# Feed-forward input loops: a gate block and its up block interleaved product by product

## The reference

```python
def swiglu_ffn(x, w_in, w_out):
    gate, up = jnp.split(x @ w_in, 2, axis=-1)
    return (jax.nn.silu(gate) * up) @ w_out

h = h + FFN_RES_WEIGHT * swiglu_ffn(rmsnorm(h, norm_ffn1[l]), ffn1_w_in[l], ffn1_w_out[l])
```

## Time and profile before

| | us |
|---|---|
| median of 3 runs | 2399.88 (2399.85 to 2400.62) |
| the profiled execution, whole time | 2398.54 |
| its span, first to last instruction | 2396.8 |
| its mean granted TensorE clock | 0.985 of full speed |

### The profile page before, as it was taken

The page is one execution under the profiler, slowest core; times in us unless marked ns, Lnnn a source line. Parts: engine busy times, 40 slices in busy tenths (PEclk is TensorE's granted clock), DMA queues, the critical chain, the costliest instruction groups (busy, mean ns, idle before and its releaser), DMA issues.

```text
span 2396.8 us, 27538 instructions
## 1 busy us (share of the span) xinstructions
PE 2303.6 (96%) x10522; PEld 1897.6 (79%) x10522; DVE 1075.4 (45%) x1093; ACT 736.1 (31%) x926; POOL 690.8 (29%) x485
## 2 busy tenths in 40 slices
PE   8999999999999999999999999997867899999997
PEld 7888888887777888888878888876767787888886
DVE  5444334534465454443454443356534435444333
ACT  4222222322323342222333222234321134322221
POOL 3444104501231034442124444011222212444300
PEclk9999999999999999999999999999989999999998
DMA  4333333333222333333333333331100012333332
GB/s 145 96 96 96 106 105 121 107 97 89 73 76 80 97 97 96 96 96 101 106 95 97 95 98 101 105 99 55 45 27 27 27 44 88 97 96 96 97 105 88
DMA packets 58817, 213.31 MB, mean 89 GB/s; under 512 B 6528, under 2 KB 6784, under 8 KB 58624
## 3 DMA queue, kind: packets, MB, share of 16 engines
q1 hardware_dynamic: 58464, 210.02, 28.3%
q0 software_dynamic: 288, 2.36, 0.3%
HBM read 210.26 MB, written 2.10 MB: 89 GB/s over the span
## 4 chain that ended last, share of the span: by engine, by line
PE 89%; DVE 4%; issue 3%; ACT 2%; POOL 2%; DMA 0%; POOLq 0%; DVEq 0%; SPq 0%
PE acc L465 27%; PE acc L466 27%; PE acc L467 27%; DVE c_acc L1636 1%; PE mixb L680 1%; PE mixb L698 1%; PE mixb L693 1%; PE mixb L860 1%; PE sums L495 1%; PE acc L804 1%; PE acc L803 1%; PE acc L802 1%; ACT w_hi L929 0%; POOL r_raw L1771 0%; PE mixb L840 0%
## 5 line engine op out<-in xcount | busy, mean ns | idle before, releaser
L465 PE MATMUL acc<-x_hi,w_hi 128*128 128x512 f32 x2016 | 803.2, 398 | 10.0 <-DVE x_lo L1262 9.0
L467 PE MATMUL acc<-x_hi,w_lo 128*128 128x512 f32 x2016 | 788.4, 391 | 0.0
L466 PE MATMUL acc<-x_lo,w_hi 128*128 128x512 f32 x2016 | 788.2, 391 | 0.0
L465 PEld LDWEIGHTS acc<-x_hi,w_hi 128*128 128x128 f32 x2016 | 381.6, 189 | 93.4 <-DVE x_lo L1262 9.4
L467 PEld LDWEIGHTS acc<-x_hi,w_lo 128*128 128x128 f32 x2016 | 380.5, 189 | 80.7
L466 PEld LDWEIGHTS acc<-x_lo,w_hi 128*128 128x128 f32 x2016 | 381.4, 189 | 78.8 <-issue 2.6
L1243 DVE TENSOR_TENSOR w_lo<-w_raw,w_hi 128x1024 fp32r<-128x1024 f32 x232 | 301.5, 1305 | 286.3 <-ACT w_hi L929 285.5
L1301 DVE TENSOR_TENSOR w_lo<-w_raw,w_hi 128x1024 fp32r<-128x1024 f32 x160 | 244.8, 1530 | 271.8 <-ACT w_hi L935 271.8
L929 ACT ACTIVATE w_hi<-w_raw 128x1024 fp32r<-128x1024 f32 x232 | 243.1, 1053 | 244.9 <-DMA w_raw<-weights 244.9
L465 PE MATMUL acc<-hid_hi,w_hi 128*128 128x512 f32 x704 | 273.9, 389 | 0.0
L466 PE MATMUL acc<-hid_lo,w_hi 128*128 128x512 f32 x704 | 273.9, 389 | 0.0
(11 more groups left out here) (307 smaller groups left out, 2061.7 us busy)
## 6 DMA issues: line engine op xcount, KB each, us to landing
w_raw<-weights SPq DMA_DIRECT2D x392, 512.0 KB, 3.5
h<-x_t SPq DMA_DIRECT2D x4, 512.0 KB, 5.9
y_t<-h SPq DMA_DIRECT2D x8, 256.0 KB, 2.2
k1c<-const POOLq DMA_DIRECT2D x1, 1536.0 KB, 7.8
k2c<-const POOLq DMA_DIRECT2D x1, 768.0 KB, 5.8
cst<-const SPq DMA_DIRECT2D x1, 161.0 KB, 7.7
vec<-vectors SPq DMA_DIRECT2D x1, 112.5 KB, 2.1
```

Of the source, the lines that this page charges most:

```text
L465: pe.matmul(bank, w_hi[:, slot, w], hi, start=start, stop=False)
L466: pe.matmul(bank, w_hi[:, slot, w], lo, start=False, stop=False)
L467: return pe.matmul(bank, w_lo[:, slot, w], hi, start=False, stop=stop)
```

## The change

TensorE's loop takes two blocks at a time. It waits until the low halves of both are counted and both banks are drained, and then runs, for each k-tile and each of the three parts, the gate block's matmul and the up block's matmul in turn, into two banks. Each of the two blocks signals `block_done` at its own last matmul, so the two signals now lie one matmul apart. The number of matmuls is the same.

ScalarE in the loop splits both next blocks before it waits for the gate's drain. VectorE makes both low halves before it waits for the first of the two blocks; the drains follow. The prologues, GpSimd's and SP's code and all other stages are as before.

```diff
                 with pe.Fori(1, 2 * KF // SLOTS) as i:
-                    for b in range(SLOTS):
-                        pe.wait_ge(lo_split, SLOTS * i + (first + b + 1))
-                        pe.wait_ge(drained, SLOTS * i + (out0 + b - 3))
+                    for b in range(0, SLOTS, 2):
+                        pe.wait_ge(lo_split, SLOTS * i + (first + b + 2))
+                        pe.wait_ge(drained, SLOTS * i + (out0 + b - 2))
                         for k in range(KD):
-                            last = product(b, k, acc[b][:, :], x_hi[:, k, :], x_lo[:, k, :], k == 0, k == KD - 1)
-                        last.then_inc(block_done, 1)
+                            w = slice(k * P, (k + 1) * P)
+                            for part, (left, right) in enumerate([(w_hi, x_hi), (w_hi, x_lo), (w_lo, x_hi)]):
+                                for up in range(2):
+                                    last = pe.matmul(acc[b + up][:, :], left[:, b + up, w], right[:, k, :],
+                                                     start=k == 0 and part == 0, stop=k == KD - 1 and part == 2)
+                                    if k == KD - 1 and part == 2:
+                                        last.then_inc(block_done, 1)
@@ ScalarE, turn_of
                     for u in range(2):
                         half_pair(2 * u, i, turn, u)
+                        half_pair(2 * u + 1, i, turn, u)
                         act.wait_ge(drained, 2 * q0 + (out0 + 2 * u + 1))
                         act.activation(f_sig[:, u, :], f_gate[:, u, :], ACT.Sigmoid).then_inc(f_sig_done, 1)
-                        half_pair(2 * u + 1, i, turn, u)
                         act.wait_ge(drained, 2 * q0 + (out0 + 2 * u + 2))
@@ VectorE, ffn
                             dve.wait_ge(hi_split, SLOTS * i + (first + b + LEAD + 1))
                             dve.tensor_tensor(w_lo[:, slot, :], w_raw[:, slot, :], w_hi[:, slot, :].bitcast(F32),
                                               ALU.subtract).then_inc(lo_split, 1)
+                        for b in (2 * u, 2 * u + 1):
                             dve.wait_ge(block_done, SLOTS * i + (first + b + 1))
```

## The result

The changed kernel takes 2415.99 us (median of four, 2414.08 to 2416.86), beside 2399.86 for the kernel before in the same runs (2399.19 to 2400.62). The ratio is 1.0066, interval 1.0054 to 1.0078: it is slower by 16.1 us.

The account below looks back on a forecast made before the run. TensorE, never waiting inside the loops, was taken to bound the kernel. Entry waits of 20.8 us plus 8.3 us of lowered clock, with 0 for products, steady loop and loop end, gave 2399.88 + 29.1 = 2429.0 us, range 2419.5 to 2434.

Parts of the forecast that it names:

- The products: In the loops of all four stages, the 3840 matmuls in the new order keep 0.2267 us each: 0.00 us.
- The rival of faster products: Alternating banks lets the 3840 loop matmuls follow sooner: at the bound of 51 us, 2378 us; chance 0.05.
- The wait at the entry: Each loop's first pair waits for block 5's low half: 5.16, 5.14, 5.35 us, fourth like second; 20.8 us in all.
- The rival "no wait": At the loop entries TensorE has no need of block 5, or VectorE is earlier: 2399.9 us; chance 0.03.
- The prediction's own sign of being wrong: At the loop entry, the prediction is wrong if block 4 starts on the heels of block 3.
- The clock: After each of four entry waits TensorE's clock falls to half: 2.1 us each, 8.3 us in all, bounds 0 and 10.2.
- The rival in which the clock holds: TensorE waits at the loop entries but no stretch at half clock follows: 2420.7 us; chance 0.08.
- The steady loop: In the loop, the chain from a pair's end to the second low half takes 9.4 us, under 10.88: costs 0.
- The sum: Over the whole kernel, 20.8 + 8.3 = 29.1 us are added to 2399.88, giving 2429.0 us.
- the forecast's own range: Whole time with entry waits and clock loss, chance 0.79: 20.8 + 6.6 to 20.8 + 10.2, 2427.3 to 2430.1 us.

Follow-up runs that it names:

- The spare products: The changed kernel with 22 and 23 spare matmuls ahead of the loop's wait in stages 0 and 2: 2410.59 us, ratio 1.0054.

## Why the prediction was right or wrong

**The products: right.** 0.2267 us was predicted, and 195.84 us for the 864 matmuls of blocks 8 to 43 is 0.2267, interleaved or not. The rival of faster products has fallen. The Trainium skill (TensorE: Matmul & The Clock Gate, "Wait — 56ns, not 53.3ns?") gives 215.7 ns for back-to-back matmuls of 512 columns at 2.4 GHz; the new order doesn't reach it.

**The wait at the entry: right in stages 0 and 2, wrong in 1 and 3. This is the step that failed.** Predicted were 5.16, 5.14, 5.35 and, for the fourth, the 5.14 of the second again; measured 5.17, none, 5.37 and none. The mechanism held wherever it applied, and its size too, though the last hundredths are luck: in the first stage the low half was done 0.07 us sooner behind block 3 than in the kernel before, and TensorE started 0.14 us behind it, not 0.05. The error is one reading: the prediction took the matmul at 882.96 as the first of block 4 in the second stage, and it is the first of block 3. The kernel before shows both matmuls at the true boundary:

```profile
888.17 0.39 PE L467 MATMUL acc<-x_hi,w_lo 128*128 128x512 f32 x1
888.40 0.39 PE L465 MATMUL acc<-x_hi,w_hi 128*128 128x512 f32 x1
```

The low half of block 5 ends at 885.80 + 2.25 = 888.05, 0.35 us before block 4 starts at 888.40. What tells the blocks apart is the sum for the norm, a matmul with a line of its own. In the first three stages of the kernel before:

```profile
21.16 1.88 PE L495 MATMUL sums<-sumsq,cst 128*128 128x512 f32 x4
...
871.17 1.02 PE L495 MATMUL sums<-sumsq,cst 128*128 128x512 f32 x2
...
1232.33 1.02 PE L495 MATMUL sums<-sumsq,cst 128*128 128x512 f32 x2
1238.68 1.02 PE L495 MATMUL sums<-sumsq,cst 128*128 128x512 f32 x2
```

From the last sum on, 24 x 0.2267 = 5.44 us make a block. 882.96 - 871.17 = 11.79 is two blocks and 0.91 us for the sum; 1250.46 - 1238.68 = 11.78 is the same, and that made the two stages look alike. But in stage 2 the last sum stands after block 1, and two blocks later is block 4; in stage 1 the only sum stands after block 0, and two blocks later is block 3. VectorE's chain hangs on the last sum: the reciprocal, the first gate, f_hid, then block 5's low half. So in stages 1 and 3 the chain starts one block, 5.44 us, earlier relative to TensorE's loop, and that is just more than the 5.14 us of wait. The kernel's text says as much (in stage 0 the sum stands after block 1 too, where the description ahead of the prediction has block 0), and I argued "the other stages show the same picture" from times that agree, without counting the blocks. The rival "no wait" was rejected for all four stages at once, by a count that says what TensorE needs and not when it is there; in two stages it was the case. The prediction's own sign of being wrong, block 4 on the heels of block 3, is what those two stages show.

**The clock: the mechanism right, two of four terms void, the size a little low.** Predicted were 2.1 us each; by the ends of block 5 it is 7.65 - 5.17 = 2.5 and 8.15 - 5.37 = 2.8. The stretches at half clock held 5.06 and 5.89 us of work; the bounds of 3.3 to 5.1 came from the two of the earlier trace rows. The spare products show the term apart: 5.4 us for two by the medians, 5.0 by the traces. The rival in which the clock holds, 2420.7 us, lies nearer to the measured time than the forecast, but by the count of waits and not by its cause: both waits have their stretch at 0.50.

**The steady loop: right.** The chain from the pair's end to the second low half was put at 9.4 us. The trace of the changed kernel, from the start of the next pair (TensorE, VectorE, GpSimd, then SP's issue):

```profile
86.14 0.62 PE L535 MATMUL acc<-x_hi,w_hi 128*128 128x512 f32 x2
97.03 0.62 PE L535 MATMUL acc<-x_hi,w_hi 128*128 128x512 f32 x2
...
86.12 0.69 DVE L1311 TENSOR_TENSOR f_gate<-acc,rstd 128x512 f32<-128x512 f32 x1 [1.59 <-PE acc L535]
90.25 0.69 DVE L1315 TENSOR_TENSOR f_hid<-acc,f_mul 128x512 f32<-128x512 f32 x1 [3.44 <-POOL f_mul L1729]
92.70 2.73 DVE L1306 TENSOR_TENSOR w_lo<-w_raw,w_hi 128x1024 fp32r<-128x1024 f32 x2 [1.75 <-ACT w_hi L940]
...
87.55 1.29 POOL L1727 TENSOR_TENSOR f_mul<-f_gate,f_sig 128x512 f32<-128x512 f32 x1 [5.24 <-ACT f_sig L979]
88.92 1.30 POOL L1729 TENSOR_TENSOR f_mul<-f_mul,rstd 128x512 f32<-128x512 f32 x1
...
86.26 0.86 SPq L454 DMA_DIRECT2D w_raw<-weights  x2
```

92.70 + 2.73 - 86.14 = 9.29 us, 1.6 before the next pair at 97.03. f_gate starts 0.02 us ahead of the next pair's first matmul, where in the kernel before it came 0.20 behind the next block's: one matmul earlier, as argued. The second multiply takes 1.30 us where it took 2.15; over 80 pairs that is 68 us, the 69 that GpSimd is busy less. In the kernel before it ran beside this low half:

```profile
107.08 1.48 DVE L1301 TENSOR_TENSOR w_lo<-w_raw,w_hi 128x1024 fp32r<-128x1024 f32 x1 [1.65 <-ACT w_hi L935]
```

The low half went on for 1.00 us of the multiply's time, until 108.56, and the multiply took 0.85 us longer; now it has no low half beside it, and the loss is gone. The Trainium skill (SBUF — State Buffer, "Who interferes with whom") has a VectorE instruction with two SBUF inputs contend with a GpSimd one that reads SBUF; the trace agrees. SP issues two loads at once. ScalarE sat idle for a load ahead of two of its 160 splits in the loops, 1.8 us in all, and TensorE waited for neither.

**The sum.** With the two waits that weren't there and their clock taken out, the prediction's own terms give 5.16 + 5.35 + 2 x 2.1 = 14.7 us, 2414.6 us; 16.1 was measured, and 1.1 of the rest is the larger clock term. The range was too narrow because each case in it had all four waits: a doubt about how many of them there are was worth 7.3 us apiece and stood nowhere. One slip changes nothing: 20.8 + 10.2 on top of 2399.88 is 2430.9, not the 2430.1 that is given as the upper end of the forecast's own range.

## What to carry to other kernels

Joining two steps moves the need of the second one forward by the length of the first: ask when the last input of the second is ready at the *entry* of every loop, where the producers are still behind, and not only in its steady state. A price found in one stage holds in another only if the order around it is the same, so anchor the count of blocks in each at a row that can't be mistaken. And price a wait of TensorE above its own length where rows of the kernel show the clock lower behind such gaps, here by half as much again (7.65 for 5.17, 8.15 for 5.37).

## What the hardware showed that I had not expected

- After a wait the second group of matmuls came later than the pace: 46.62 - 46.03 = 0.59 us for two at full clock, where two take 0.45, and 41.15 - 40.14 = 1.01 at half clock, where the 12 matmuls of 5.06 us have 0.84 for two. It costs some 0.15 us, once for each wait.
- A spare GpSimd multiply that takes 1.30 us alone adds 1.26 us behind another one (2.55 for two).
- The mixing stage of the second block took 430.8 to 434.7 us in traces of kernels that don't differ in it. TensorE was busy in it for 364.8 to 368.9 us, the other engines for the same times within 0.3 us: what differs is which of its matmuls fell in stretches at half clock. Whole spans of single traces can't be compared to better than that, which is more than some of the terms here.
